# Value products as paired plain fp32, a second gate weight buffer, and compressed scores with both key parts in one product

## The chip, the cores and the metric

The kernel is one program on one core of one Trainium2 chip. Its engines are TensorE (PE in the profile, with its weight loads as PEld), VectorE (DVE), ScalarE (ACT), GpSimd (POOL) and the queue of SyncE (SP), which issues the DMAs. Each has its own list of instructions, worked off in order, and they meet at semaphores. The metric is the time of one launch on the device, in microseconds (us), from the median of several runs.

## The reference, cut to what matters

One decoder layer over 512 tokens of width 1024, all in fp32. Attention has 16 heads of 64 dims: eight block-sparse ones (MoBA; at this length every token sees its own and the earlier block, so they are causal attention) and eight NSA heads in two groups. An NSA head adds three branches: over 31 compressed blocks (`cmp`), over selected blocks (`slc`) and over a window (`win`), each with a gate of its own.

```python
h = rms_norm(x, attn_norm)
(mq, mk, mv, nsq, kc, vc, ksl, vsl, kwn, vwn, ngate, mgate) = split(h @ w_in)
y_a = softmax(q k^T * SCALE + bias) @ v                      # 8 MoBA heads
p_cmp = masked_softmax_safe(q kc^T * SCALE + bias)           # 31 compressed keys
o = gates[0] * (p_cmp @ vc) + gates[1] * o_slc + gates[2] * o_win   # 8 NSA heads
g_a, g_b = split(sigmoid(mgate))                             # 2 x 1024 columns
x = x + (g_a * (y_a @ w_br_moba) + g_b * (y_b @ w_br_nsa)) @ w_o
x = x + (gelu(conv_a) * conv_b) @ w_down                     # conv of rms_norm(x) @ w_up
x = x + sigmoid(x @ w_ple_gate) * (p @ w_ple)
```

## The kernel before, in words

**Arithmetic.** Most products are made of fp32r operands. Each fp32 operand is split into a high part (a copy rounded to fp32r) and a low part (the rest), and `three` (lines 1514 to 1518) issues high x high, high x low and low x high into one PSUM bank: three TensorE instructions for a product. Weights are split as they come in: the high part on ScalarE or VectorE, the low part on VectorE and GpSimd. Transposes and a few small products use plain fp32 operands (`L1604` for the hidden layer of the compression, `L1615` for its output, `L1701` for the warm-up). A plain fp32 product that is no transpose is one instruction in the program and two MATMUL records in the trace.

**Stages.** A prologue normalises and transposes x, projects the first head groups and compresses keys and values. Then comes attention, a loop over 100 steps (`STEPS`). After it the branch matrices, `w_o`, the FFN and the last gate follow as one stream of weight chunks.

**Attention.** Heads go in eight pairs `n` (0 to 3 MoBA, 4 to 7 NSA), two heads `e` in each. A unit `u` is one head and one branch: four steps, one for each block `i` of 128 queries, against 128*(i+1) keys. A MoBA pair has 2 units (8 steps), an NSA pair 4 units and one `cmp` step for both heads (17 steps). A step's chain: `scores` (PE) fills a bank, `bias` (DVE, L1301) adds the bias and takes the row minimum, `exp` (ACT, L900), `invert` (DVE, L1318), `scale` (POOL, L711 or L714); three steps later `turn_probs` (PE, L1667) transposes the probabilities, `pt_high` (ACT, L925, `cmp`: L922) copies them out of PSUM as the high part, `pt_low` (DVE, L1336, `cmp`: L1332) makes the low part. Two steps after the unit's last transposes, `values` (PE) multiplies: 4 key blocks x `three`, over 512, 384, 256 and 128 query columns. All products of a pair add up in bank 6, heads on different partitions: the stationary operand is always 128 wide, 64 columns of values and 64 of zeros, so that one head's product adds zeros to the other's half.

The values themselves are split by `v_high` (ACT, L866 for MoBA, four times L872 for an NSA pair) and `v_low` (POOL, L688, or four times L693).

**Compressed scores.** For each of 4 query blocks and 2 heads, `scores` makes two products of 32 columns, with the high keys `KCh` and the low keys `KCl` (L1641, L1642): 16 instructions per `cmp` step.

**Work between.** TensorE fills the steps with the projections of the next pairs (`PROJ`) and with 14 of the 16 blocks of the merge gates (`GATE`, L1516 to L1518 on bank 7; in pairs 6 and 7 a gate is 24 matmuls spread over four steps, then two steps without gate work follow). There is one gate weight buffer, `Gh`/`Gl`. At the step after gate `j` ends, ScalarE empties bank 7 (`take_gate`, L932) and then writes `Gh` for gate `j+1` (L1013), and VectorE (L1200) and GpSimd (L679) each make half of `Gl`. Gate `j+1` waits for that.

**Order.** Nothing is scheduled by a planner: the tables `PROJ`, `SPLIT`, `VALUES`, `GUESS`, `ROOT`, `TILE`, `TURN`, `GATE`, keyed by step, say at which step each engine does what beside the softmax chain.

## Time and profile before

| | |
|---|---|
| median of 3 runs | 921.58 us |
| lowest, highest | 920.68, 921.92 us |
| the profiled execution | 921.52 us |
| its span, first to last instruction | 919.7 us |
| TensorE clock granted, mean | 0.996 |
| attention loop | about 88 to 394 us of the span |
| TensorE busy in it | 286.9 of 306 us |

The profiled execution is as long as the median (0.06 us less), and 1.8 us of it lie outside the span. Rows of the trace give the start and length of instructions. A matmul's length includes its latency, and the next one starts before it ends: what a matmul costs in a dense stream is the distance from its start to the next start.

### The profile page before, as it was taken

How to read it: one execution, taken by the hardware profiler on the slowest of the kernel's cores; microseconds unless marked ns; L12 is line 12 of the kernel's file. 1: busy time of each engine (PE TensorE's matmuls, PEld its weight loads, DVE VectorE, ACT ScalarE, POOL GpSimd, SP SyncE). 2: the span in 40 equal slices, each digit the busy share in tenths (PEclk: the TensorE clock that was granted, in tenths of full speed). 3: DMA queues.
4: the chain of work that ended last, by engine and by line, in shares of the span. 5: the costliest groups of instructions: out<-in, count | busy, mean ns of one | idle time of the engine just before them, and what ended most of it. 6: DMA issues, size and time to landing. Idle time of an engine off the chain costs nothing.

```text
span 919.7 us, 13404 instructions
## 1 busy us (share of the span) xinstructions
PE 884.6 (96%) x4601; PEld 764.8 (83%) x4601; DVE 423.9 (46%) x961; ACT 411.8 (45%) x893; POOL 437.0 (48%) x557
## 2 busy tenths in 40 slices
PE   7999899999899799999999999999999999999998
PEld 7899699999798687877788888888888888888886
DVE  4545665767755654545413644444444440021124
ACT  5224555665646454634333544444444442231321
POOL 4740644664634342656462464444444445444450
PEclk9999999999999999999999999999999999999999
DMA  5845423333121223456532453333333333322213
GB/s 175 198 116 149 104 62 101 93 75 87 47 58 47 58 71 113 138 192 207 180 120 80 157 153 92 103 91 92 92 99 97 97 98 108 99 94 91 92 58 137
DMA packets 101366, 99.33 MB, mean 108 GB/s; under 512 B 15956, under 2 KB 76084, under 8 KB 101300
## 3 DMA queue, kind: packets, MB, share of 16 engines
q1 hardware_dynamic: 101247, 98.48, 36.5%
q8 instruction: 38, 0.62, 0.3%
q14 instruction: 28, 0.23, 0.1%
q10 hardware_dynamic: 53, 0.01, 0.0%
HBM read 87.58 MB, written 10.88 MB: 107 GB/s over the span
## 4 chain that ended last, share of the span: by engine, by line
PE 85%; DVE 5%; ACT 4%; issue 3%; POOL 2%; DMA 1%; SPq 0%; ACTq 0%; DVEq 0%; POOLq 0%
PE banks L1516 25%; PE banks L1517 25%; PE banks L1518 25%; PE banks L1667 2%; PE banks L1647 1%; PE banks L1646 1%; PE banks L1576 1%; PE banks L1604 1%; ACT split_arena L1013 1%; DMA plain_arena<-gates 1%; DMA plain_arena<-in_conv_w_dram 1%; ACT split_arena L889 1%; PE banks L1701 1%; DVE plain_arena L1301 1%; DVE split_arena L1200 1%
## 5 line engine op out<-in xcount | busy, mean ns | idle before, releaser
L1516 PE MATMUL banks<-split_arena 128*128 128x512 f32 (+4 forms) x1228 | 463.1, 377 | 12.8 <-DVE split_arena L1200 6.2
L1518 PE MATMUL banks<-split_arena 128*128 128x512 f32 (+4 forms) x1228 | 453.4, 369 | 0.0
L1517 PE MATMUL banks<-split_arena 128*128 128x512 f32 (+4 forms) x1228 | 453.3, 369 | 0.0
L699 POOL TENSOR_TENSOR split_arena<-plain_arena,split_arena 128x512 fp32r<-128x512 f32 x184 | 241.1, 1322 | 254.8 <-ACT split_arena L941 235.2
L1516 PEld LDWEIGHTS banks<-split_arena 128*128 128x128 f32 x1228 | 231.1, 188 | 50.9 <-DVE split_arena L1200 7.2
L1518 PEld LDWEIGHTS banks<-split_arena 128*128 128x128 f32 x1228 | 230.7, 188 | 35.4
L1517 PEld LDWEIGHTS banks<-split_arena 128*128 128x128 f32 x1228 | 231.3, 188 | 31.9
L941 ACT ACTIVATE split_arena<-plain_arena 128x512 fp32r<-128x512 f32 x184 | 113.0, 627 | 193.2 <-PE banks L1518 179.1
L1474 DVE SCALAR_TENSOR_TENSOR plain_arena<-banks,plain_arena 128x511 f32<-128x511 f32 x44 | 32.7, 743 | 133.2 <-ACT plain_arena L1053 133.2
L900 ACT ACTIVATE plain_arena<-plain_arena 128x128 f32<-128x128 f32 (+1 forms) x96 | 54.0, 562 | 52.7 <-DVE plain_arena L1301 52.4
L714 POOL TENSOR_SCALAR plain_arena<-plain_arena 128x128 f32<-128x128 f32 (+1 forms) x64 | 41.0, 641 | 74.4 <-DVE plain_arena L1318 74.4
L925 ACT ACTIVATE split_arena<-banks 128x128 fp32r<-128x128 f32 (+1 forms) x96 | 41.5, 433 | 66.7 <-PE banks L1667 57.9
L1301 DVE CUSTOM_DVE_ANT_0 plain_arena<-banks,plain_arena 128x128 f32<-128x128 f32 (+1 forms) x96 | 46.7, 486 | 47.0 <-PE banks L1647 46.8
L1336 DVE TENSOR_TENSOR split_arena<-banks,split_arena 128x128 fp32r<-128x128 f32 (+1 forms) x96 | 46.2, 482 | 15.1 <-ACT split_arena L925 14.0
L1667 PE MATMUL banks<-plain_arena 128*128 128x128 f32 x240 | 43.1, 278 | 2.4 <-DVE split_arena L1336 1.5
L1492 DVE TENSOR_TENSOR plain_arena<-banks,plain_arena 128x512 f32<-128x512 f32 x8 | 5.0, 683 | 86.5 <-PE banks L1518 86.5
L711 POOL TENSOR_SCALAR plain_arena<-plain_arena 128x128 f32<-128x128 f32 (+3 forms) x32 | 21.6, 674 | 46.2 <-DVE plain_arena L1318 45.7
L679 POOL TENSOR_TENSOR split_arena<-plain_arena,split_arena 128x512 fp32r<-128x512 f32 x16 | 26.6, 1665 | 35.3 <-DVE split_arena L1195 22.2
L675 POOL TENSOR_TENSOR split_arena<-plain_arena,split_arena 128x384 fp32r<-128x384 f32 (+1 forms) x28 | 31.3, 1122 | 19.6 <-ACT split_arena L841 10.1
L1053 ACT ACTIVATE plain_arena<-banks,plain_arena 128x512 f32<-128x512 f32 x44 | 30.6, 777 | 22.0 <-PE banks L1518 22.0
L1476 DVE SCALAR_TENSOR_TENSOR plain_arena<-banks,plain_arena 128x510 f32<-128x510 f32 x44 | 32.9, 749 | 1.5
L1667 PEld LDWEIGHTS banks<-plain_arena 128*128 128x128 f32 x240 | 28.8, 142 | 5.1 <-POOL plain_arena L714 3.1
(170 smaller groups left out, 821.7 us busy)
## 6 DMA issues: line engine op xcount, KB each, us to landing
plain_arena<-in_w_up_dram SPq DMA_DIRECT2D x88, 256.0 KB, 3.1
plain_arena<-in_w_down_dram SPq DMA_DIRECT2D x44, 256.0 KB, 2.6
plain_arena<-in_w_in_dram SPq DMA_DIRECT2D x18, 512.0 KB, 4.3
plain_arena<-in_w_in_dram SPq DMA_DIRECT2D x32, 192.0 KB, 4.2
plain_arena<-in_x_dram SPq DMA_DIRECT2D x8, 512.0 KB, 5.4
gates<-plain_arena SPq DMA_DIRECT2D x16, 256.0 KB, 2.0
plain_arena<-skew SPq DMA_DIRECT2D x16, 256.0 KB, 3.9
plain_arena<-gates SPq DMA_DIRECT2D x16, 256.0 KB, 4.2
```

Of the source, the lines that this page charges most:

```text
L699: pool.tensor_tensor(W2l[:, c % RING, :], raw2[:, c % RING, :], W2h[:, c % RING, :].bitcast(F32), ALU.subtract).then_inc(w2_lo, 1)
L714: pool.tensor_scalar(p_, p_, r, gsig[:, s["i"], h:h + 1], ALU.mult, ALU.mult).then_inc(scaled, 1)
L900: nc.scalar.activation(prob[:, t % 4, 0:nk], prob[:, t % 4, 0:nk], ACT.Exp, bias=mneg[:, t % 4:t % 4 + 1], scale=-1.0, accum_out=rsum[:, t ...
L925: nc.scalar.activation(PTh[:, s["u"] % 2, 0:i + 1, P * i:P * (i + 1)], PS[:, 4 + t % 2, 0:P * (i + 1)].rearrange("p (j q) -> p j q", j=i + ...
L941: nc.scalar.activation(W2h[:, c % RING, :], raw2[:, c % RING, :], ACT.Copy).then_inc(w2_hi, 1)
L1301: nc.vector.tensor_tensor_reduce(out=prob[:, t % 4, 0:nk], in0=PS[:, 2 + t % 2, 0:nk], in1=strip[:, n % 2, e, S - nk:S], scale=1.0, scalar ...
L1336: nc.vector.tensor_tensor(PTl[:, s["u"] % 2, 0:i + 1, P * i:P * (i + 1)], PS[:, 4 + t % 2, 0:P * (i + 1)].rearrange("p (j q) -> p j q", j= ...
L1476: nc.vector.scalar_tensor_tensor(out=dst[:, f % 2, 2:S], in0=PS[:, b, 0:S - 2], scalar=cst[:, CONVW + col:CONVW + 1 + col], in1=dst[:, f % ...
L1516: nc.tensor.matmul(o, ah, bh, start=first, stop=False)
L1517: nc.tensor.matmul(o, ah, bl, start=False, stop=False)
L1518: return nc.tensor.matmul(o, al, bh, start=False, stop=last)
L1667: ins = nc.tensor.transpose(PS[:, 4 + t % 2, P * j:P * (j + 1)], prob[:, t % 4, P * j:P * (j + 1)], ident)
```

## The change

The order of the steps changes: within a pair the branch is now the outer loop and the head the inner one, so both heads of a branch follow each other. A unit's values are no longer multiplied alone. `values` runs once for two units (`due`), on both heads. Its operands are plain fp32: `pt_low`, `v_high` and `v_low` are gone, ScalarE copies the probabilities as they are (`take_probs`, into four slots instead of two), and GpSimd copies the values once per pair (`take_values`). For each key block there are two matmuls of 64 output rows each, one head to partitions 0 to 63 and the other to partitions 64 to 127 of bank 6. The compressed values are one plain fp32 product instead of a `three`.

The gate weights get two buffers, taken in turn, and are split one gate earlier: at the end of gate `j` the weights of `j+2` are split, and one more split (gate 3) and one more load (gate 4) stand at steps 1 and 2. The compressed keys lie high and low side by side, so that one product of 64 columns gives both parts; VectorE adds them with one more instruction per `cmp` step.

```diff
-        for e in range(2):
-            for br in (["own"] if n < 4 else ["slc", "win"]):
+        for br in (["own"] if n < 4 else ["slc", "win"]):
+            for e in range(2):
...
-                if j > 0:
-                    dve.wait_ge(gate_filled, j)
-                nc.vector.tensor_copy(Gh, graw).then_inc(g_hi, 1)
+                if j > 1:
+                    dve.wait_ge(gate_filled, j - 1)
+                nc.vector.tensor_copy(Gh[j % 2], graw).then_inc(g_hi, 1)
...
                     if t == end + 1:
                         take_gate(j)
-                        if j + 1 < NGATE:
-                            act.wait_ge(graw_in, 16 * (j + 2))
-                            nc.scalar.activation(Gh, graw, ACT.Copy).then_inc(g_hi, 1)
+                        if j + 2 < NGATE:
+                            gate_high(j + 2)
+                if t == 1:
+                    gate_high(3)
...
+            def take_values(w):
                 n = w - 1
+                pool.wait_ge(qkv_done, 4 * w + 4)
+                if n >= 4:
+                    pool.wait_ge(pv_done, (n - 4) // 2 + 1)
+                pool.tensor_copy(V[:, vslot(n)], qkv[:, :, 256:384]).then_inc(v_done, 1)
...
-                            oq = o[:, P * q + 32 * e:P * q + 32 * e + 32]
-                            nc.tensor.matmul(oq, QQ[qslot(n)][:, e, P * q:P * (q + 1)], KCh[:, g, :], start=True, stop=False)
-                            ins = nc.tensor.matmul(oq, QQ[qslot(n)][:, e, P * q:P * (q + 1)], KCl[:, g, :], start=False, stop=True)
+                            oq = o[:, P * q + 64 * e:P * q + 64 * e + 64]
+                            ins = nc.tensor.matmul(oq, QQ[qslot(n)][:, e, P * q:P * (q + 1)], KC[:, g, :], start=True, stop=True)
...
-                    ins = three(PS[:, 6, :], VCh[:, g, :], VCl[:, g, :], PTh[:, u % 2, 0, :], PTl[:, u % 2, 0, :], False, closing)
+                    ins = nc.tensor.matmul(PS[:, 6, :], VC[:, (n - 4) // 2, :], PT[:, u % 4, 0, :], start=False, stop=closing)
                 else:
-                    vs = vslot(n, s["br"])
-
-                    for j in (reversed(range(NT)) if closing else range(NT)):
-                        q = slice(P * j, S)
-                        ins = three(PS[:, 6, q], Vh[:, vs, j, c0:c0 + P], Vl[:, vs, j, c0:c0 + P], PTh[:, u % 2, j, q], PTl[:, u % 2, j, q],
-                                    opening and j == 0, closing and j == 0)
+                    for j in range(NT):
+                        for h in range(2):
+                            c0 = DH * (h if n < 4 else s["br"] == "win")
+                            ins = nc.tensor.matmul(PS[DH * h:DH * (h + 1), 6, P * j:S], V[:, vslot(n), j, c0:c0 + DH], PT[:, (u - 1 + h) % 4, j, P * j:S],
+                                                   start=opening and j == 0, stop=closing and j == NT - 1)
                 ins.then_inc(pv_done, 1)
```

TensorE in an NSA pair, the value products. Before, this piece stands after each unit; it is one unit of one head, twelve matmuls on all 128 output rows.

```order
L1516 MATMUL banks<-split_arena 128x512
L1517 MATMUL banks<-split_arena 128x512
L1518 MATMUL banks<-split_arena 128x512
L1516 MATMUL banks<-split_arena 128x384
L1517 MATMUL banks<-split_arena 128x384
L1518 MATMUL banks<-split_arena 128x384
L1516 MATMUL banks<-split_arena 128x256
L1517 MATMUL banks<-split_arena 128x256
L1518 MATMUL banks<-split_arena 128x256
L1516 MATMUL banks<-split_arena 128x128
L1517 MATMUL banks<-split_arena 128x128
L1518 MATMUL banks<-split_arena 128x128
```

The same place in the changed kernel, with the scores (L1612, L1613) and the transposes (L1633) of the running step ahead of it.

```order
L1612 MATMUL banks<-attention_split 128x128
L1613 MATMUL banks<-attention_split 128x128
L1633 MATMUL banks<-plain_arena 128x128 x2
L1655 MATMUL banks<-attention_plain 64x512 x2
L1655 MATMUL banks<-attention_plain 64x384 x2
L1655 MATMUL banks<-attention_plain 64x256 x2
L1655 MATMUL banks<-attention_plain 64x128 x2
```

Twelve matmuls per unit, 24 for two heads, have become eight for both heads, each of 64 output rows, and they stand at every second place only.

GpSimd in steps 1 to 3 of attention, in the kernel before: the last of the root iterations (L724 to L730), scales (L711), low parts of the projection weights (L675) and of the values (L688).

```order
L728 TENSOR_SCALAR plain_arena<-plain_arena 128x8
L730 TENSOR_TENSOR plain_arena<-plain_arena 128x8
L711 TENSOR_SCALAR plain_arena<-plain_arena 128x256
L675 TENSOR_TENSOR split_arena<-plain_arena,split_arena 128x384
L688 TENSOR_TENSOR split_arena<-plain_arena,split_arena 128x4x2x64
L711 TENSOR_SCALAR plain_arena<-plain_arena 128x384
L675 TENSOR_TENSOR split_arena<-plain_arena,split_arena 128x384
```

The same in the changed kernel (L681 is the gate's low part, L704 the scale, L677 the projection weights, L688 the copy of the values).

```order
L721 TENSOR_SCALAR plain_arena<-plain_arena 128x8
L723 TENSOR_TENSOR plain_arena<-plain_arena 128x8
L681 TENSOR_TENSOR attention_split<-plain_arena,attention_split 128x512
L704 TENSOR_SCALAR plain_arena<-plain_arena 128x256
L677 TENSOR_TENSOR split_arena<-plain_arena,split_arena 128x384
L688 COPY attention_plain<-plain_arena 128x512
L704 TENSOR_SCALAR plain_arena<-plain_arena 128x384
L677 TENSOR_TENSOR split_arena<-plain_arena,split_arena 128x384
```

The gate's low part now stands ahead of the scale of step 1 and of the projection weights of step 2; the subtraction on the values has become a copy.

## Rows read from the trace of the kernel before

**Rows 1.** The page: busy time by engine (us, share of span, instructions).

```profile
PE 884.6 (96%) x4601; PEld 764.8 (83%) x4601; DVE 423.9 (46%) x961; ACT 411.8 (45%) x893; POOL 437.0 (48%) x557
```

**Rows 2.** Busy time by stretch: length, then each engine's busy us, PE clock, DMA share.

```profile
88.00:116.00 28.00, 23.55 (x134) 20.89 (x133) 17.71 (x47) 16.46 (x42) 16.45 (x36) 1.00 0.44 117
116.00:207.00 91.00, 90.55 (x550) 84.85 (x549) 61.14 (x170) 54.93 (x149) 50.00 (x109) 1.00 0.34 83
207.00:302.00 95.00, 87.92 (x553) 79.52 (x552) 60.03 (x198) 55.60 (x162) 45.19 (x97) 1.00 0.20 58
302.00:394.00 92.00, 84.91 (x489) 73.44 (x489) 51.98 (x178) 52.32 (x145) 38.33 (x49) 0.98 0.30 95
```

**Rows 3.** Waits of PE, 88 to 394 us: us in total, times, longest.

```profile
PE banks L1516 <- DVE split_arena L1200: 6.2, 5, 1.5
PE banks L1576 <- DVE plain_arena L1268: 5.2, 4, 2.8
PE banks L1516 <- DVE split_arena L1184: 3.1, 2, 1.7
```

**Rows 4.** Timeline of PE, one value unit (start, us, line, form, count).

```profile
151.51 0.48 PE L1516 MATMUL banks<-split_arena 128*128 128x512 f32 x1
151.83 0.39 PE L1517 MATMUL banks<-split_arena 128*128 128x512 f32 x1
152.06 0.40 PE L1518 MATMUL banks<-split_arena 128*128 128x512 f32 x1
152.30 0.33 PE L1516 MATMUL banks<-split_arena 128*128 128x384 f32 x1
...
153.45 0.39 PE L1516 MATMUL banks<-split_arena 128*128 128x384 f32 x1
```

**Rows 5.** Timeline of PE, plain fp32 products of the compression.

```profile
53.60 3.68 PE L1604 MATMUL banks<-plain_arena 128*128 128x62 f32 x32
...
74.38 0.34 PE L1518 MATMUL banks<-split_arena 128*128 128x384 f32 x1
74.65 0.63 PE L1615 MATMUL banks<-plain_arena 128*31 128x64 f32 x8
```

**Rows 6.** Timeline of PE, one step of compressed scores (first, last, next).

```profile
308.53 0.26 PE L1641 MATMUL banks<-split_arena 128*128 128x32 f32 x1
...
310.21 0.26 PE L1642 MATMUL banks<-split_arena 128*128 128x32 f32 x1
310.32 0.44 PE L1667 MATMUL banks<-plain_arena 128*128 128x128 f32 x2
```

**Rows 7.** Timeline of all engines at a gate that waits for its weights.

```profile
312.23 0.62 ACT L932 ACTIVATE plain_arena<-banks 128x512 f32<-128x512 f32 x1
...
312.71 1.08 ACT L1013 ACTIVATE split_arena<-plain_arena 128x1024 fp32r<-128x1024 f32 x1
...
314.57 0.50 PE L1516 MATMUL banks<-split_arena 128*128 128x512 f32 x1 [1.43 <-DVE split_arena L1200]
```

**Rows 8.** Timeline of POOL and PE at the longest wait.

```profile
294.55 2.83 POOL L693 TENSOR_TENSOR split_arena<-plain_arena,split_arena 128x256 fp32r<-128x256 f32 x4 [1.64 <-ACT split_arena L872]
297.35 0.67 POOL L714 TENSOR_SCALAR plain_arena<-plain_arena 128x384 f32<-128x384 f32 x1
...
302.16 1.09 PE L1576 MATMUL banks<-plain_arena 128*128 128x128 f32 x4 [2.84 <-DVE plain_arena L1268]
```

**Rows 9.** Groups by line: busy us, mean ns of one, idle before.

```profile
L1336 DVE TENSOR_TENSOR split_arena<-banks,split_arena 128x128 fp32r<-128x128 f32 (+1 forms) x96 | 46.2, 482 | 15.1 <-ACT split_arena L925 14.0
L900 ACT ACTIVATE plain_arena<-plain_arena 128x128 f32<-128x128 f32 (+1 forms) x96 | 54.0, 562 | 52.7 <-DVE plain_arena L1301 52.4
L925 ACT ACTIVATE split_arena<-banks 128x128 fp32r<-128x128 f32 (+1 forms) x96 | 41.5, 433 | 66.7 <-PE banks L1667 57.9
L679 POOL TENSOR_TENSOR split_arena<-plain_arena,split_arena 128x512 fp32r<-128x512 f32 x16 | 26.6, 1665 | 35.3 <-DVE split_arena L1195 22.2
L807 POOL COPY plain_arena<-plain_arena 128x512 f32<-128x512 f32 x1 | 0.6, 612 | 2.2 <-ACT plain_arena L1096 2.2
```

198 lines of the change are left out of this document (79 added, 119 removed).

## Prediction

> **What bounds the kernel now.** First the busy times of the page [rows 1]: TensorE is busy 884.6 of 919.7 us, no other engine over 48%. Busy time of a matmul includes latency, so this alone doesn't prove a bound. Next the attention loop by stretches [rows 2]: 286.9 of 306 us, with 0.45 us free between 116 and 207 us and some 4.5, 7 and 7 us in the other three. So TensorE sets the pace in attention, with about 19 us of holes. Then the waits of TensorE [rows 3]: 6.2 us of them are for the low part of gate weights (L1200), 5.2 us for the normalised queries and keys (L1268), 3.1 us for projection weights (L1184). What follows attention is the same stream of chunks in both kernels, and I give it no change: all terms lie in attention, and one that shortens TensorE's list there, or a wait of it, moves the end by as much, until a softmax chain comes last instead.
>
> **Value products, before.** One unit runs from 151.51 us to the next product at 153.45 us: 1.94 us for twelve matmuls [rows 4]. The 512-column ones follow each other at 0.235 us. There are 4 x 2 + 4 x 4 = 24 units: 46.6 us.
>
> **Value products, after.** Twelve calls (4 MoBA pairs, 2 for each of 4 NSA pairs), each 4 key blocks x 2 heads = 8 plain fp32 matmuls, which is 16 records, since a plain fp32 product leaves two. No row before shows a plain record of 512 columns. The bounds: the small product of the compression makes 8 records of 64 columns in 0.63 us [rows 5]. Less the last one's latency of about 0.22 that is 0.41 over 7 distances, 0.058 us for 64 columns, or 0.9 ns a column; fp32r takes 0.235 / 512 = 0.46 ns [rows 4]. One end is therefore the fp32r pace (0.235 us for 512 columns), the other twice that. The other rows of plain products don't decide it: 32 records of 62 columns take (3.68 - 0.27) / 31 = 0.11 us each [rows 5], as much as the 32-column fp32r records with their 128-wide weights [rows 6], so the weight load sets those. I take the slow end, 0.45, 0.34, 0.23 and 0.12 us for 512, 384, 256 and 128 columns, because L1615 is the only row in which the weights (31 wide) are too small to set the pace. A head's 8 records then take 2 x 1.14 = 2.28 us.
>
> The second unknown is whether the two heads' matmuls overlap, as they use different output rows of the array. Nothing before overlaps in that way. Fully overlapped, a call takes 2.28 us; if the records start in order, the second head begins one record late and a call takes 2.28 + 0.45 = 2.73 us; in series it takes 4.56 us. I take 2.5 us, and 0.2 us for two changes of the array's shape: from the last fp32r product to the first 31-wide one there are 0.27 us where 0.17 is the usual step [rows 5]. So 12 x 2.7 = 32.4 us, a gain of **14.2 us**. In series it would be 12 x 4.76 = 57.1 us, a loss of 10.5 us. Why the overlap rather than the series: weight loads of one product already run beside the streaming of another (PEld is busy 764.8 us beside PE's 884.6 [rows 1]), so the array isn't one unit that a single instruction holds; but that is thin, and the series stays a rival. The Trainium skill, TensorEngine Tiling (Array Packing), section Tiling Modes, says that a 128x64 shape makes two tiles that load and multiply in parallel, and that changing the shape drains the engine; no run here shows the former. By it a call would be near 2.28 us plus the drains.
>
> **Compressed scores.** 16 records in 310.32 - 308.53 = 1.79 us, 0.112 each whatever their columns [rows 6]. Eight remain: 4 x 8 x 0.112 = **3.6 us** gained. VectorE gets one more addition per `cmp` step, 4 of some 0.45 us in all the loop, beside other work. **Compressed values:** three fp32r matmuls of 512 (0.70 us) become two plain records (0.90 at the slow end, 0.47 at the fast): **0.8 us** lost over four steps.
>
> **Gate weights.** At a gate's end ScalarE empties bank 7 (0.62 us, from 312.23), writes the high part (1.08 us), VectorE the low one, and TensorE starts at 314.57 after 1.43 us idle [rows 7]. With two buffers the weights of the next gate are ready by then, and the same instructions work for the one after it. All 6.2 us [rows 3] go: what is late next is the scores' chain, 0.6 (bias) + 0.75 (exp) + 0.16 + 0.65 (scale) = some 2.3 us against three steps, and a gate's first part of 1.4 us now covers it. Gain **6.2 us**. ScalarE's and SyncE's waits keep their lead: the load for gate j+2 is issued as many steps ahead of its split as before.
>
> **Less beside TensorE.** VectorE loses 96 low parts of 0.482 us, 46.2 us [rows 9], 15% of its time in the loop; they stood between the transposes and the next but one. At 294.55 GpSimd spends 2.83 us on four low parts of values, after 1.64 us waiting for ScalarE's high parts, and then the scale at 297.35 and the root iterations, the result of which TensorE awaits until 302.16 (2.84 us idle) [rows 8]. One copy of 0.61 us [L807, rows 9] takes their place: over 2 us sooner for that chain. TensorE arrives sooner there too, so I count only about half of the 5.2 + 3.1 us of such waits: **3 us** gained (bounds 0 and 8).
>
> **What it adds.** Gate 3 is now split at step 1: 1.66 us on GpSimd [L679, rows 9], 1.06 on ScalarE, 0.7 on VectorE. Queued behind it on GpSimd are the scale of step 1, a projection weight's low part and the first values; TensorE waits for the scale in step 4 and for the weights in the projection from step 4 on. This is the stretch from 88 to 116 us, where TensorE is free 4.5 of 28 us already [rows 2], so it isn't hidden well: **1.5 us** lost (bounds 0 and 2.8). The copy of the values (0.61 instead of 1.3 us) pays part of it back. Load 4 at step 2 holds SyncE's queue until gate 3's low part is made, with the raw weights of later projections behind it; those have several steps of lead.
>
> **Steps that get too short.** ScalarE needs 0.562 + 0.19 + 0.433 = 1.2 us a step [L900, L925, rows 9] and 1.7 us at each gate's end; TensorE's steps without gate, projection or values hold some 0.7 us, with values they held 1.9 more. Between bursts that now come at every eighth step rather than every fourth, short steps stand in a row. From 302 us on, ScalarE is busy 52.3 of 92 us [rows 2], so there is no bound on the mean, but I take off **4 us** of the 24 us of gains (bounds 0 and 8).
>
> **Sum.** 14.2 + 3.6 - 0.8 + 6.2 + 3 - 1.5 - 4 = 20.7 us. The profiled execution took 921.5 us, the same as the median: 921.5 - 20.7 = 900.8, say **901 us**.
>
> **Rivals.**
> *In series.* The two heads' matmuls don't overlap, and the pairing does nothing: -10.5 + 3.6 - 0.8 + 6.2 + 3 - 1.5 and no loss to short steps: 0.0, 921.5 us. For it: no row shows an overlap. Against it: nothing but weight loads running beside products.
> *Slower.* In series, and the weight loads of a 64-wide tile aren't hidden either. Such a load is half of the 0.11 us of a 128-wide one [rows 6]: 16 x 0.055 x 12 = 10.6 us more, 932 us. It decides as soon as more than about 0.04 us of each record's load shows. Against it: before, a stream of 512-column products goes at 0.235 us with a load in each [rows 4], of which nothing shows. The Trainium skill, TensorE: Matmul & The Clock Gate, section Part 3: Packing small matmuls, says that loads overlap matmuls in flight only when their row group differs, and here both heads use all rows. Before, all products use all rows and their loads do overlap, so the trace disagrees with it for full-width tiles.
> *Faster.* A plain record streams at the fp32r pace and the heads overlap: a call is 1.14 + 0.23 + 0.2 = 1.6 us, 13 us less, 888 us. Against it: L1615 [rows 5].
> *The softmax chain takes over.* The pairing works but the short steps give back twice what I took off and the early split costs 2.8 us: 906 us. This is inside my forecast's own range, 895 to 909.
>
> **Chances.** Forecast with its range 0.68, in series 0.18, slower 0.08, faster 0.06. Within 0.2% is what a measurement of this kernel can tell from no change: 919.7 to 923.4 us. In series falls on either side of that: 0.06 faster, 0.08 within, 0.04 slower. So faster 0.80, same 0.08, slower 0.12. The range goes from 891 (part of the faster case) to 922 us (the series).
>
> **What would show it.** The trace after should have plain 64-row products with starts of the second head's record within 0.05 us of one of the first head's, and about 2.7 us from a call's first record to the product behind it; 4.6 us would mean the series. Waits of TensorE for the gate's low part should be gone. The `cmp` scores should take 0.9 us. DVE's busy time should fall by about 47 us. The wait at 302 us should shrink, and its dip of the clock with it. Wrong would be: a pace of the plain records other than 0.45 us for 512 columns, waits of the transposes (for the scale) of more than 8 us in sum, or a new hole of several us before 116 us.

## The result, and the profile after

The changed kernel took **914.6 us** (912.67 to 917.26, four runs) against 921.75 us for the kernel before beside it: ratio 0.993, 95% interval 0.9915 to 0.9946. The change gains 7.1 us, about a third of the 20.7 us of the sum. The profiled execution is the slowest of the four, 917.26 us with a span of 915.3 us, so its trace shows only 4.3 us of gain; the readings below are differences inside the two traces, held against that.

The page after, busy time by engine, answers to [rows 1]:

```profile
PE 878.3 (96%) x4469; PEld 735.4 (80%) x4469; DVE 378.0 (41%) x864; ACT 406.7 (44%) x880; POOL 426.9 (47%) x547
```

VectorE lost 45.9 us, TensorE 6.3 us. The stretches of attention, answering to [rows 2] (length, busy us of PE, PEld, DVE, ACT and POOL, PE clock, DMA share, GB/s):

```profile
88.00:116.00 28.00, 22.50 (x118) 19.97 (x117) 15.63 (x41) 15.12 (x37) 17.43 (x37) 0.94 0.48 127
116.00:207.00 91.00, 90.57 (x550) 80.83 (x548) 50.40 (x154) 55.59 (x152) 48.01 (x112) 1.00 0.37 91
207.00:295.00 88.00, 82.88 (x504) 68.80 (x503) 45.30 (x161) 53.01 (x154) 40.74 (x89) 0.98 0.20 57
295.00:385.00 90.00, 78.49 (x422) 60.70 (x423) 37.64 (x146) 53.78 (x149) 39.25 (x49) 0.95 0.31 98
```

Two things are new: in the last 90 us TensorE is free for 11.5 us (7.1 of 92 before), and its granted clock is below 1.00 in three of four stretches. Together the clock column stands for 28 x 0.06 + 88 x 0.02 + 90 x 0.05 = 7.9 us of lost pace, against 92 x 0.02 = 1.8 us before. The window ends at 385 us and misses most of the last stretch at the lower clock, 383.7 to 387.1 us. With it there are five such stretches of 3.4 us in attention, 17.1 us in all, of which half is lost: 8.5 us, against one stretch and 1.7 us before. The waits of TensorE from 88 to 385 us, answering to [rows 3] (us in total, times, longest):

```profile
PE banks L1483 <- ACT plain_arena L911: 5.7, 3, 2.1
PE banks L1543 <- DVE plain_arena L1248: 4.8, 4, 2.0
PE banks L1483 <- POOL split_arena L790: 4.6, 1, 4.6
PE banks L1483 <- DVE split_arena L1164: 2.8, 2, 2.2
```

The gate's low part (L1200 before) is gone from the list. In its place stand L911, ScalarE emptying the gate's bank 7, with 5.7 us, and L790, GpSimd's first low part of y, with one wait of 4.6 us at the end of attention. L1248 and L1164 are the lines that were L1268 and L1184.

A call of the paired value products in the timeline of TensorE (start, us, form, count), answering to [rows 4]:

```profile
136.41 0.40 PE L1633 MATMUL banks<-plain_arena 128*128 128x128 f32 x2
136.74 2.38 PE L1655 MATMUL banks<-attention_plain 128*64 128x512 f32 x16
139.05 0.44 PE L1483 MATMUL banks<-split_arena 128*128 128x384 f32 x1
```

From 136.74 to 139.05 us are 2.31 us for both heads; all twelve calls take 2.30 or 2.31. A plain fp32 product leaves two records, here called its first and second pass. Inside a call the records start in pairs, 7 ns apart: the first pass of both heads, then the second pass of both. A pass of 512 columns takes 0.43 us to the next start. And the compressed scores, answering to [rows 6]:

```profile
300.64 1.06 PE L1608 MATMUL banks<-attention_split 128*128 128x64 f32 x8
301.53 0.33 PE L1633 MATMUL banks<-plain_arena 128*128 128x128 f32 x1
```

0.89 us, as forecast. So both mechanisms of the change work as described; what became of their gain is the question of the experiments.

Why TensorE waits for L911, in the timeline of all engines after (in brackets: idle before, and what ended it):

```profile
301.53 0.77 PE L1633 MATMUL banks<-plain_arena 128*128 128x128 f32 x5
301.74 0.42 DVE L1289 TENSOR_TENSOR plain_arena<-banks,plain_arena 128x256 f32<-128x256 f32 x1 [0.94 <-PE banks L1608]
...
303.11 0.42 DVE L1292 TENSOR_TENSOR plain_arena<-plain_arena 128x256 f32<-128x256 f32 x1
...
303.57 0.42 ACT L876 ACTIVATE plain_arena<-plain_arena 128x256 f32<-128x256 f32 x1 [0.29 <-DVE plain_arena L1292]
...
303.89 0.58 ACT L911 ACTIVATE plain_arena<-banks 128x512 f32<-128x512 f32 x1
...
304.61 0.47 PE L1483 MATMUL banks<-split_arena 128*128 128x512 f32 x1 [2.14 <-ACT plain_arena L911]
```

The bank has been full since about 299.5 us. ScalarE empties it only behind the exponential L876 of the compressed step, which waits for VectorE's four-operation bias chain (L1289 to L1292, one addition longer than before), which waits for the scores. Before the change the same order held, but the low part of the next weights came later still, and hid it.

Behind attention the kernels were to be equal. They aren't. The groups of matmuls in the dn stage, before (748 to 870 us) and after (740 to 865 us), columns as in [rows 9]:

```profile
L1516 PE MATMUL banks<-split_arena 128*128 128x512 f32 x177 | 69.0, 390 | 0.0
```

```profile
L1483 PE MATMUL banks<-late_arena,split_arena 128*128 128x512 f32 x176 | 69.6, 396 | 0.0
```

A matmul is 6 ns longer on average; from start to start it is 233.5 ns instead of 226.7, and the stage takes 123.3 us instead of 119.8. In the up stage, with the same shape, both kernels go at 226.7 ns (239.5 us). From the first transpose of x to the up stage it is 81.5 instead of 80.3 us. So 4.7 us go behind attention.

### The profile page after: what moved, and what is told of

It reads as the page before. It is cut to its first block, busy times and chain, and to the rows that moved or that the text cites. A ratio compares the mean times of both kernels' runs of the same rounds, so it can differ in the third digit from the quotient of the medians.

```text
span 915.3 us, 13019 instructions
## 1 busy us (share of the span) xinstructions
PE 878.3 (96%) x4469; PEld 735.4 (80%) x4469; DVE 378.0 (41%) x864; ACT 406.7 (44%) x880; POOL 426.9 (47%) x547
## 4 chain that ended last, share of the span: by engine, by line
PE 86%; DVE 4%; ACT 3%; issue 3%; POOL 2%; DMA 1%; SPq 1%; ACTq 0%; DVEq 0%; POOLq 0%
PE banks L1483 25%; PE banks L1485 25%; PE banks L1484 25%; PE banks L1655 3%; PE banks L1633 2%; PE banks L1613 1%; PE banks L1612 1%; PE banks L1543 1%; PE banks L1571 1%; PE banks L1663 1%; DMA plain_arena<-in_conv_w_dram 1%; ACT attention_split L868 1%; DVE plain_arena L1281 0%; ACT plain_arena L879 0%; POOL split_arena L677 0%
## 5 line engine op out<-in xcount | busy, mean ns | idle before, releaser
L692 POOL TENSOR_TENSOR split_arena<-plain_arena,split_arena 128x512 fp32r<-128x512 f32 x184 | 240.9, 1321 | 263.3 <-ACT split_arena L925 243.7
L1483 PE MATMUL banks<-split_arena 128*128 128x512 f32 (+3 forms) x808 | 305.6, 378 | 12.4 <-POOL split_arena L790 4.6
L1485 PE MATMUL banks<-split_arena 128*128 128x512 f32 (+3 forms) x808 | 297.7, 368 | 0.0
L1484 PE MATMUL banks<-split_arena 128*128 128x512 f32 (+3 forms) x808 | 297.3, 368 | 0.0
L1483 PEld LDWEIGHTS banks<-split_arena 128*128 128x128 f32 x808 | 152.8, 189 | 38.2 <-POOL split_arena L790 4.8
L1485 PEld LDWEIGHTS banks<-split_arena 128*128 128x128 f32 x808 | 152.7, 189 | 21.5
L1484 PEld LDWEIGHTS banks<-split_arena 128*128 128x128 f32 x808 | 153.1, 189 | 20.3 <-issue 0.5
L1483 PE MATMUL banks<-late_arena,split_arena 128*128 128x512 f32 x240 | 95.2, 397 | 0.0
L1485 PE MATMUL banks<-late_arena,split_arena 128*128 128x512 f32 x240 | 94.8, 395 | 0.0
L1484 PE MATMUL banks<-late_arena,split_arena 128*128 128x512 f32 x240 | 94.8, 395 | 0.0
L707 POOL TENSOR_SCALAR plain_arena<-plain_arena 128x128 f32<-128x128 f32 (+1 forms) x64 | 40.8, 639 | 72.3 <-DVE plain_arena L1299 72.3
L904 ACT ACTIVATE attention_plain<-banks 128x128 f32<-128x128 f32 (+1 forms) x96 | 41.6, 433 | 69.6 <-PE banks L1633 69.4
L1485 PEld LDWEIGHTS banks<-late_arena,split_arena 128*128 128x128 f32 x240 | 45.0, 187 | 11.1
L1484 PEld LDWEIGHTS banks<-late_arena,split_arena 128*128 128x128 f32 x240 | 45.0, 187 | 10.8
L1483 PEld LDWEIGHTS banks<-late_arena,split_arena 128*128 128x128 f32 x240 | 45.0, 188 | 10.8
L1633 PE MATMUL banks<-plain_arena 128*128 128x128 f32 x240 | 43.2, 281 | 1.2 <-POOL plain_arena L707 1.2
L677 POOL TENSOR_TENSOR split_arena<-plain_arena,split_arena 128x384 fp32r<-128x384 f32 (+1 forms) x28 | 32.7, 1173 | 22.5 <-ACT split_arena L836 12.9
```

The lines of the kernel that those rows point to most:

```text
L677: pool.tensor_tensor(Wl[:, kt, 0:c], raw[:, kt, 0:c], Wh[:, kt, 0:c].bitcast(F32), ALU.subtract).then_inc(w_lo[1], 1)
L692: pool.tensor_tensor(W2l[:, c % RING, :], raw2[:, c % RING, :], W2h[:, c % RING, :].bitcast(F32), ALU.subtract).then_inc(w2_lo, 1)
L707: pool.tensor_scalar(p_, p_, r, gsig[:, s["i"], h:h + 1], ALU.mult, ALU.mult).then_inc(scaled, 1)
L904: nc.scalar.activation(PT[:, u % 4, 0:i + 1, P * i:P * (i + 1)], PS[:, 4 + t % 2, 0:P * (i + 1)].rearrange("p (j q) -> p j q", j=i + 1), A ...
L1483: nc.tensor.matmul(o, ah, bh, start=first, stop=False)
L1484: nc.tensor.matmul(o, ah, bl, start=False, stop=False)
```

## The experiments

Each comparison of times is with the kernel before on the same chip; the kernel after is 914.6 us throughout. For each run the trace also gives, from the first scores to the first transpose of x, the sum of TensorE's gaps of 0.35 us or more and the time at the lower clock (1.2 GHz, seen in pieces of 3.4 us; a piece that begins within 0.3 us of that transpose is counted). Half of such a piece is lost where TensorE works through it, and less where it waits anyway. Both columns come from one execution each:

| kernel | us | ratio to before, 95% | gaps | us at 1.2 GHz |
|---|---|---|---|---|
| before | 921.8 | | 21.4 | 3.4 |
| after | 914.6 | 0.9915 to 0.9946 | 22.8 | 17.1 |
| a_serial | 931.6 | 1.0094 to 1.0131 | 21.0 | 13.7 |
| a_onegate | 921.9 | 0.9992 to 1.0027 | 26.5 | 30.7 |
| a_gate3late | 915.3 | 0.9917 to 0.9947 | 22.4 | 23.9 |
| a_takefirst | 909.7 | 0.9862 to 0.9903 | 20.7 | 13.7 |
| b_takefirst | 922.1 | 0.9999 to 1.0018 | 20.7 | 13.7 |
| a_invfirst | 914.9 | 0.9917 to 0.9944 | 21.2 | 23.9 |
| a_ylow | 915.2 | 0.9905 to 0.9942 | 21.8 | 20.5 |
| a_endgap | 912.6 | 0.9881 to 0.9921 | 20.1 | 17.1 |
| a_align | 912.5 | 0.989 to 0.994 | 22.1 | 13.7 |
| b_shift | 921.9 | 0.9995 to 1.0026 | 20.4 | 10.2 |
| a_rel14272 | 910.7 | 0.9861 to 0.9912 | 23.4 | 17.1 |
| a_best | 904.9 | 0.9793 to 0.9835 | 18.8 | 10.2 |
| a_best2 | 902.9 | 0.9781 to 0.9825 | 19.0 | 13.7 |
| a_best3 | 900.6 | 0.9754 to 0.9784 | 16.2 | 10.2 |

The last column changes between executions of the same instructions. b_shift only places the data elsewhere and has two pieces that the trace of before lacks; a_ylow differs from the kernel after only at the end of attention, and yet has a piece at 98 us that the kernel after lacks. One or two pieces (1.7 or 3.4 us of time) between two rows are therefore not shown to come from the edit. That the change as such lowers the clock is better founded: its four runs have a mean granted clock of 0.988 to 0.991, and 47 runs of the kernel before have 0.992 to 0.998.

### Is it the pairing? a_serial

```diff
-                    for j in range(NT):
-                        for h in range(2):
+                    for h in range(2):
+                        for j in range(NT):
```

> The kernel after, with the value products of a call in the order of the heads: all four key blocks of the first head (output rows 0 to 63), then all four of the second (rows 64 to 127), instead of the two heads in turn. The same 8 products and 16 records a call. Theory E (two products run side by side only when they stand next to each other and differ in their 64 columns of the array): a call takes twice as long, 4.4 us or a little more instead of 2.3 us, TensorE's stream grows by 12 x 2.1 = 25 us, and the time is 20 to 27 us above the kernel after (935 to 941 us), which is the prediction's rival in series with its 4.6 us a call. Rival F (plain products into 64 rows are cheap in themselves, side by side or not): a call stays at 2.3 to 2.7 us and the time at 914 to 918 us.

931.55 us, 16.9 us above the kernel after. The call:

```profile
136.66 3.93 PE L1655 MATMUL banks<-attention_plain 128*64 128x512 f32 x16
140.52 0.44 PE L1483 MATMUL banks<-split_arena 128*128 128x384 f32 x1
```

3.86 us instead of 2.31. Theory E holds in kind: the same records take 1.55 us less when the two heads stand next to each other, 12 x 1.55 = 18.6 us in all. In size it missed: the call isn't twice as long, because at the one seam a rest of the overlap is there: the second head's two 512-column passes start beside the first head's last 256-column and 128-column ones. The second head's eight records alone take 2.30 us, as long as the whole paired call. Without the pairing the change would have cost 10 us.

### Is it the gates split one gate earlier? a_onegate

```diff
-                    if t == end + 1 and j + 2 < NGATE:
-                        split_gate(j + 2)
-                if t == 1:
-                    split_gate(3)
+                    if t == end + 1 and j + 1 < NGATE:
+                        split_gate(j + 1)
```

(and the same on SyncE, ScalarE and VectorE; both weight buffers stay)

> The kernel after, with the gate weights loaded and split one gate ahead, as in the kernel before, instead of two (no split of gate 3 at step 1), into the same two alternating buffers. By the prediction, two gates ahead is worth 6.2 us of waits less 1.5 us for the early split: this kernel would be 4.7 us slower than the kernel after (919 us). By the traces since, where the waits for the low part have given way to waits for the emptying of bank 7 and for the scale chain: within 1.5 us of the kernel after. If the early split does more harm than the second buffer good, it is faster than the kernel after, and the two gaps of TensorE from 98 to 108 us are smaller.

921.86 us: 7.3 us slower than after, and the same as before. From the first scores to the first transpose of x it is 3.1 us shorter than the kernel before (335.7 for 338.8 us), where the kernel after is 9.2 us shorter; the slower pace behind attention, below, takes the 3.1 us and more. TensorE's list in attention, counted from start to start without gaps and without what the lower clock adds, falls from 315.0 to 295.6 us there, about as in the kernel after (296.7 us). But its gaps of any length are 5.5 us longer than before and the lower clock costs 10.8 us more, so 3 of 19 us are left. The waits of TensorE in that kernel:

```profile
PE banks L1475 <- DVE attention_split L1174: 8.8, 4, 3.7
PE banks L1475 <- POOL split_arena L786: 4.6, 1, 4.6
PE banks L1475 <- DVE split_arena L1174: 4.5, 2, 3.7
```

The low part of the gate weights (L1174 here) now costs 13.3 us where it cost 6.2 [rows 3], and four of the gaps have 6.8 us at the lower clock behind them. The work on ScalarE and VectorE ahead of a gate is the same, but TensorE arrives sooner, since its list is shorter. My 1.5 us "by the traces since" was wrong, since I had compared with before's 6.2 us; the prediction's 4.7 us were nearer, and also too small. No run has the two gate buffers without the rest of the change, so what they would gain alone on the kernel before is not shown.

### The early split: a_gate3late

```diff
-                if t == 1:
-                    split_gate(3)
+                if t in (4, 8):
+                    split_gate(3 if t == 4 else 4)
```

(and the same on the other engines; from step 10 on as in the kernel after)

> The kernel after, with the weights of gates 3 and 4 split at steps 4 and 8 instead of 1 and 4; from step 10 on two gates ahead as in the kernel after. Theory I (the early split of gate 3 is what opens the 2.0 and 2.25 us gaps at 98 and 106 us, by keeping GpSimd from the roots of the normalisation): the gaps of TensorE from 95 to 110 us fall from 5.5 us to the 3.8 us of the kernel before or less, and the time falls by 1 to 3 us against the kernel after (912 to 913.5 us). Rival J (the work only moves, to a gap behind step 8): the same sum of gaps up to 130 us and the same time within 1 us.

915.32 us, no change. Theory I was right on the place: the gaps from 95 to 110 us are 0.72, 1.75 and 0.66, sum 3.1 us instead of 5.5. A new one of 1.15 us appears at 125 us, behind step 8, as in rival J. And behind the same two gaps of 2.1 and 4.6 us at the end there are now 6.8 us at the lower clock each, not 3.4, which in this execution takes the rest back. Alone the edit shows no gain.

### What took the gate's place: a_takefirst and b_takefirst

```diff
             for t in range(T + LAG):
+                for j, end in gate_end.items():
+                    if t == end + 1:
+                        take_gate(j)
                 for done in proj_end(t):
...
                     if t == end + 1:
-                        take_gate(j)
```

> The kernel after, with ScalarE emptying the gate's bank at the start of the step behind the gate's end, ahead of that step's copies of probabilities and its exponential, instead of behind them. Theory C (the emptying of bank 7 is what is late where the low part of the weights had been): TensorE's 5.7 us of waits for L911 go to under 1 us, at least two of the five dips of the clock in attention go with them (each costs some 1.7 us), and the time falls by 3 to 6 us against the kernel after. Rival D (the wait only covers another: the scores' chain, behind which ScalarE stood, is late as well): the waits turn up at the transposes or score banks, the sum of the gaps of TensorE from 15 to 400 us stays at 22 to 25 us, and the time changes by less than 1.5 us either way.

909.65 us, 5.0 us under the kernel after: theory C. The waits for the emptying are gone, and at the place quoted above TensorE now goes on after 0.40 us:

```profile
301.76 0.66 PE L1635 MATMUL banks<-plain_arena 128*128 128x128 f32 x4 [0.40 <-POOL plain_arena L707]
302.17 0.47 PE L1485 MATMUL banks<-split_arena 128*128 128x512 f32 x1
```

The lower clock behind the gaps near 237, 305 and 343 us is gone in this execution, though 3.4 us more stand at the end of attention and 3.4 us near 411 us. Part of rival D holds too: the waits for L1250 (the normalised vectors) rise from 4.8 to 6.4 us.

> The kernel before, with ScalarE emptying the gate's bank at the start of the step, ahead of its other work (the edit of a_takefirst, on the kernel without the change). If that edit is worth as much there, 5 us (916 us), the gain of a_takefirst has nothing to do with the change. By the traces: in the kernel before TensorE waited at the gates for the low part of the weights, 6.2 us, which is made behind the high part that stands behind the emptying; taking it first moves the high part little, so the gain should be 0 to 2 us (919 to 922 us).

922.07 us, 0.9999 to 1.0018 of before: the edit is worth nothing there. So the emptying of the bank became late only through the change.

### The gap at the end of attention: a_invfirst, a_ylow, a_endgap

Instructions of three engines stand in front of the first product behind attention. These runs moved them one after the other: VectorE's reciprocals ahead of the bias in compressed steps; then GpSimd's first low part of y ahead of the last scale and of a fill; then VectorE's low part of y behind the last bias.

```diff
+                early = 1 <= t < T and STEPS[t]["br"] == "cmp"
+                if early:
+                    invert(t - 1)
                 if t < T:
                     bias(t)
-                if 1 <= t <= T:
+                if 1 <= t <= T and not early:
                     invert(t - 1)
```

> The kernel after, with VectorE taking the reciprocals of the step before ahead of the bias chain in the five-operation steps of the compressed branch (4 steps), instead of behind it. Theory G (the 4.58 us gap of TensorE at the end of attention is that reciprocal: GpSimd's scale waits for it, and the last low parts of y stand behind the scale on GpSimd): that gap falls by 1.5 to 2 us, to 2.5 to 3 us, and the time by 1 to 3 us against the kernel after (912 to 913.5 us). Rival H (the gap is ScalarE's high parts or GpSimd's own work, 4 x 0.6 us and more): the gap stays over 4 us and the time within 1 us of the kernel after.

914.86 us; the gap falls from 4.58 to 3.82 us, half of what theory G wanted, and it is still GpSimd that ends it. No gain.

```diff
+                if t == T - 1:
+                    pool.wait_ge(gate_filled, NGATE)
+                    pool.wait_ge(yt_hi, 1)
+                    pool.tensor_tensor(yTl[:, 0, :], ytmp[:, 0, :], yTh[:, 0, :].bitcast(F32), ALU.subtract).then_inc(yt_lo[0], 1)
                 if t >= 1:
                     scale(t - 1)
```

> The kernel after, with GpSimd writing the first low part of y (needed by the first product behind attention) ahead of the scale of the last but one step, instead of behind that scale and behind a fill that waits for the bias of the last step. Theory K (the 4.6 us gap at the end of attention is the queue in front of that one instruction: reciprocal, scale, bias of the compressed step, fill): the gap falls from 4.6 to under 2 us, the time by 2.5 to 5 us against the kernel after (910 to 912 us), the half-speed stretch of the clock behind it with it. Rival L (the next thing, ScalarE's high part of y or the scores' chain of the last steps, is nearly as late): the gap stays over 3 us, the time within 1.5 us of the kernel after.

915.2 us; rival L. The gap is 3.96 us and has another last waiter, the emptying of the last gate's bank, again behind the exponential of the compressed step:

```profile
381.10 0.47 PE L1486 MATMUL banks<-split_arena 128*128 128x512 f32 x1 [3.96 <-ACT plain_arena L914]
```

With that emptied first (a_best2, below), the gap is still 4.03 us, and the timeline shows the next in line:

```profile
368.60 1.27 POOL L767 TENSOR_TENSOR split_arena<-plain_arena,split_arena 128x512 fp32r<-128x512 f32 x1 [0.73 <-ACT split_arena L1012]
369.01 1.41 DVE L1375 TENSOR_TENSOR split_arena<-plain_arena,split_arena 128x512 fp32r<-128x512 f32 x1 [1.90 <-ACT split_arena L1012]
370.35 0.15 DVE L1304 RECIPROCAL plain_arena<-plain_arena 128x1 f32<-128x1 f32 x1
370.42 0.40 DVE L1294 TENSOR_TENSOR plain_arena<-banks,plain_arena 128x256 f32<-128x256 f32 x1
...
371.77 1.12 DVE L1297 TENSOR_TENSOR plain_arena<-plain_arena 128x256 f32<-128x256 f32 x1
...
373.23 0.76 PE L1491 MATMUL banks<-split_arena 128*128 128x512 f32 x1 [4.03 <-DVE plain_arena L1297]
```

The last bias chain (L1294 to L1297) had its scores at 368.6 us, and stood behind VectorE's own low part of y, which takes 1.41 us beside GpSimd's and 0.69 alone.

```diff
-                if T - 2 <= t < T + 1:
-                    m = 2 * (t - T + 2) + 1
+                for m in {T - 1: (1, 3), T: (5,)}.get(t, ()):
```

> The kernel after with the edits of a_invfirst and a_ylow and one more: VectorE writes its low part of y (1.4 us there, since GpSimd works beside it) behind the last bias chain instead of ahead of it. Theory M (the gap at the end of attention is the bias chain of the last step, which stood in VectorE's queue behind the low part of y; with 4.6, 3.8 and 4.0 us in turn three queues were equally late): the gap falls from 4.0 to about 2.5 us or less, with one stretch of half clock behind it less, and the time by 2 to 5 us against the kernel after (910 to 912.5 us). Rival N (the emptying of the gate's bank on ScalarE, or the product's own operands, are as late again): the gap stays over 3.5 us and the time at 914 to 916 us.

912.62 us with all three moves: the gap is 2.73 us, and the lower clock behind it is gone (another piece stands at 99 us instead, so their sum is that of the kernel after). Theory M, at the low end of its gain: 2.0 us, and the intervals of the two kernels still overlap. ScalarE's emptying of the bank ends this gap, and in a_best3, where that is first, 1.96 us are left:

```profile
372.07 0.47 PE L1490 MATMUL banks<-split_arena 128*128 128x512 f32 x1 [1.96 <-DVE plain_arena L1297]
```

So the 4.6 us had four causes, each hidden behind the one in front: GpSimd's queue, the reciprocals, the emptying of the bank and VectorE's low part of y. The first two, each removed alone, brought no time.

### The pace behind attention: a_align, b_shift, a_rel14272

```diff
-        F = ctx.enter_context(nc.sbuf_tensor("plain_arena", [P, 14280], F32))
+        F = ctx.enter_context(nc.sbuf_tensor("plain_arena", [P, 14288], F32))
```

> The kernel after, with plain_arena 8 columns (32 bytes a partition) longer, so that attention_plain, attention_split and late_arena begin at a multiple of 64 bytes instead of 32 bytes past one. Nothing else changes. Theory A (start of the moving operand): in the dn stage, whose moving operand gT stands in late_arena, the three matmuls of a product follow each other at 234 ns in the kernel after and at 227 ns in the kernel before, 1/32 of 213 ns apart, as if a 512-column operand that begins 32 bytes off took one 64-byte piece more. By it this kernel's dn stage takes 119.8 us instead of 123.3 us, the wo stage about 1 us less, and the whole is 4 to 6 us under the kernel after (about 909 to 911 us). Rival B (the operand's place in another arena, far up in memory, or the drained state after attention, costs the 7 ns): dn stays at 234 ns and 123.3 us, and the time stays at 914 to 917 us.

912.5 us. The dn stage takes 121.0 us: its three matmuls follow each other at 232, 226 and 229 ns. In part what theory A wanted.

The kernel before with plain_arena ahead of split_arena:

```diff
-        R = ctx.enter_context(nc.sbuf_tensor("split_arena", [P, 38912], F32R))
         F = ctx.enter_context(nc.sbuf_tensor("plain_arena", [P, 14280], F32))
+        R = ctx.enter_context(nc.sbuf_tensor("split_arena", [P, 38912], F32R))
```

> The kernel before, with plain_arena laid out ahead of split_arena, so that split_arena, which holds nearly all moving operands of TensorE, begins 32 bytes past a multiple of 64. Nothing else changes. Theory A (start of the moving operand): every fp32r product of 512 columns takes some 6.7 ns more, dn goes from 119.8 to about 123.3 us and up from 239.5 to about 246.5 us, the whole is 15 to 24 us slower than before (937 to 946 us). Rival B (it is another property of the new arenas): no stage changes, within 1 us of 921.6 us.

921.91 us, dn 119.8, up 239.5 us: no stage moved, although every moving operand in split_arena now begins 32 bytes past a multiple of 64. Theory A is wrong: the start alone doesn't matter.

```diff
-        F = ctx.enter_context(nc.sbuf_tensor("plain_arena", [P, 14280], F32))
+        F = ctx.enter_context(nc.sbuf_tensor("plain_arena", [P, 14272], F32))
```

> The kernel after, with plain_arena 8 columns shorter (14272, its last columns are unused), so that late_arena begins 122,624 bytes behind split_arena: a multiple of 256 bytes. In the kernel after that distance is 122,656 (96 modulo 128), in the run with aligned arenas 122,688 (64 modulo 128). In the kernel before gT and the ring of weights stood in one arena, 32,768 bytes apart, with or without the shift of the whole arena. Theory A2 (what counts is the distance in memory between the moving operand gT and the weights read beside it, modulo 128 bytes or more, not either's own start): the dn stage returns to 226 or 227 ns a matmul and 119.8 us, the whole is 3 to 5 us under the kernel after (910 to 912 us). Rival B (late_arena as such costs something): dn stays at 121 to 123.3 us.

910.67 us (two runs, 908.75 and 912.6), 3.9 us under the kernel after; the stages show it more surely than the times. The same group as above:

```profile
L1483 PE MATMUL banks<-late_arena,split_arena 128*128 128x512 f32 x176 | 68.6, 389 | 0.0
```

dn takes 119.8 us, and the stretch ahead of the up stage 80.2 us, both as before. Three distances between gT and the ring of its weights are thus measured: 32 modulo 128 bytes (233.5 ns a matmul; 122,656 is 32 modulo 128, and the 96 in the expectation is a slip), 64 (229), 0 (226.7). In the kernel before and in b_shift the distance is 0 modulo 128 too, at 226.7 ns. In these five placements the pace goes with the distance, and no start of the moving operand alone explains it. That it is the weight reads beside the stream that collide is my reading, which no run shows.

### All of it: a_best, a_best2, a_best3

a_best has four edits: plain_arena at 14272 columns, the gate's bank first, the reciprocals first, the later splits of gates 3 and 4. a_best2 adds the move on GpSimd, a_best3 the one on VectorE.

> The kernel after, with four things at once: plain_arena 8 columns shorter (as in a_rel14272), ScalarE emptying the gate's bank first (as in a_takefirst), the reciprocals ahead of the compressed branch's bias (as in a_invfirst), and the weights of gates 3 and 4 split at steps 4 and 8 instead of 1 and 4, from step 10 on two gates ahead as in the kernel after. If the separate gains add up: 5 us for the bank, 3 us for dn, 1.5 us for the last gap, 1 to 2 us for the hole near 100 us: 903 to 906 us. If the gaps only move, as they did between the gate's waits, and the dips of the clock stay: 907 to 910 us.

> The kernel of a_best with the first low part of y ahead of the scale, as in a_ylow. In a_best the gap at the end of attention was still 3.8 us, with a stretch of 6.8 us at half clock behind it. By theory K both shrink: 899 to 902 us. By rival L: 903 to 905 us, as a_best.

> The kernel of a_best2 with VectorE's low part of y behind the last bias chain. Here the gate's bank is emptied first already, and the last bias was what TensorE waited for (4.0 us, with 6.8 us of half clock behind it). By theory M: the gap 2.5 us or less, 899 to 901.5 us. By rival N: 902 to 904 us.

904.86, 902.86 and 900.57 us. Made together, the edits give more than alone: the four of a_best gave 5.0 and 3.9 us and nothing in single runs, and 9.7 us here. a_best3 is 14.0 us under the kernel after and 2.3% under before (0.9754 to 0.9784), the best of all kernels here. Its last two stretches of attention:

```profile
207.00:295.00 88.00, 82.90 (x504) 68.64 (x502) 45.90 (x160) 53.17 (x154) 40.40 (x88) 0.98 0.18 53
295.00:372.00 77.00, 71.99 (x405) 54.46 (x403) 34.98 (x135) 49.08 (x139) 36.52 (x45) 1.00 0.34 108
```

5.0 us are free in the last stretch instead of 11.5, at the full clock. a_best2 missed theory K (its gap stayed at 4.0 us, as told above); a_best3 hit theory M.

## Why the prediction failed, by its own steps

What bounds the kernel was read rightly, and so was the direction; 914.6 us lies inside the range and outside the forecast's own 895 to 909.

**Value products.** -14.2 us forecast. A call takes 2.305 us and its first record starts 0.20 us behind the last transpose, where a 128-wide product starts 0.03 us behind one, so the shape change costs 0.17 us: 12 x 2.48 = 29.7 us for 46.6, **-16.9 us**. The pace of 0.43 us for 512 columns is near the slow end I took (0.45), and the overlap is complete, where I had taken 2.5 us, between overlapped (2.28) and one record late (2.73). The Trainium skill, TensorEngine Tiling (Array Packing), section Tiling Modes, which the prediction weighed, says that different tiles load and multiply in parallel and that a change of the mode drains the engine; the records 7 ns apart and the 0.17 us agree with both.

**Compressed scores** -3.6 us, as measured. **Compressed values**: 0.46 us a step instead of the 0.90 taken, about -1 us instead of +0.8.

**Gate weights, -6.2 us: the step that failed first.** "What is late next is the scores' chain ... and a gate's first part of 1.4 us now covers it" left out an instruction that the prediction itself had named a few sentences earlier, ScalarE emptying bank 7. It stood in ScalarE's queue behind that very chain, so it inherits the chain's lateness in full. L1200's 6.2 us went and L911's 5.7 us came: **-0.5 us** at this point. But the term's meaning was also wrong: a_onegate shows the earlier split, which the second buffer allows, to be worth 7.3 us in the changed kernel, not against the waits of before but against those that the shorter stream would have made. The terms for pairing and gates were added as if independent, and they aren't: without the earlier split the pairing leaves 3.1 us in attention. That most of what the split gains is the pairing's is argued from this; the split without the pairing was not run.

**Less beside TensorE, -3 us.** The waits for normalised vectors outside the first hole fell from 5.2 to 2.8 us: **-2.4 us**. The chain at 295 us came sooner, as read from [rows 8].

**Early split, +1.5 us**: the gaps from 95 to 110 us grew from 3.8 to 5.5 us, **+1.7**, and moving the split alone gained nothing.

**Steps too short, +4 us: mis-sized.** The gap at the end of attention grew from 1.3 to 4.6 us, +3.3, and the lower clock costs 8.5 instead of 1.7 us, +6.8: **+10.1 us**. I had written that the dip of the clock would shrink with the wait near 302 us. That wait did shrink, to 1.2 us at 295 us, and its dip went. But there is now a dip behind each of five other gaps of 1.4 to 4.6 us, at 111, 237, 305, 343 and 384 us. A gap doesn't always bring one: none follows the gap of 2.0 us at 101 us, nor any of seven gaps of 1.3 to 1.7 us in the trace of before. What decides it is not shown. The granted clock (last but two of the columns) behind two of the gaps:

```profile
305.00:309.00 4.00, 4.00 (x15) 3.42 (x14) 2.63 (x10) 1.98 (x6) 2.22 (x2) 0.57 0.29 83
343.00:346.50 3.50, 3.50 (x13) 2.92 (x13) 2.47 (x8) 1.56 (x4) 1.78 (x1) 0.55 0.23 82
```

**Behind attention, 0: wrong by 4.7 us.** "What follows attention ... I give it no change" took the same instructions for the same time. The change had moved gT and mT to another arena; a_rel14272 gives 3.9 us back by moving it 32 bytes. Why the distance counts stays open.

The sum of what was found is -16.9 - 3.6 - 1.0 - 0.5 - 2.4 + 1.7 + 10.1 + 4.7 = -7.9 us, against -7.1 measured by the medians and -4.3 between the two profiled executions, from which these terms are read. So 3.6 us are not placed. Most of them lie in TensorE's list in attention, which got 18.3 us shorter (315.0 to 296.7 us) and not 16.9 + 3.6 + 1.0 = 21.5. That the sum comes near the medians is luck: the profiled execution of the kernel after is the slowest of its four.

**The rivals.** In series was wrong (2.3 us a call, not 4.6), though its result, 921.5 us, is what a_onegate took, for another reason. "The softmax chain takes over" at 906 us was the right kind, and too small. What would show it: VectorE's 46 us, the compressed scores and the lost waits for the low part came as said. The sum of the waits for the scale rose only from 0.8 to 1.2 us (L714, then L707), so this warning sign didn't come: it wasn't the scale that was late, but an unrelated instruction queued behind the chain.

## What to carry to other kernels

When TensorE's list gets shorter between two of its waits, those waits can grow by as much, up to the next engine's chain (here from 6.2 to 13.3 us in a_onegate): price a shorter list and a removed wait together, and ask for each wait that goes what stands right behind it in each queue, first of all the instructions that empty a bank and have nothing to do with the chain ahead of them. Such instructions belong at the head of a step's queue; moving this one was worth 5 us after the change and nothing before it. And when a change lays out the memory anew, compare the start-to-start pace of one untouched stage before adding up the terms.

## What the runs showed of the hardware

- Plain fp32 products into output rows 0 to 63 and 64 to 127, issued in turn, run fully side by side: 16 records in 2.31 us, as long as one head's 8 records alone (2.30 us in a_serial), against 3.86 us when one head's follow the other's.
- The pace of a 512-column fp32r product went with the distance between the moving operand and the weights that are loaded beside it: 226.7 ns at 0, 229 at 64 and 233.5 at 32 modulo 128 bytes. A shift of both together changes nothing. The Trainium skill, TensorE: Matmul & The Clock Gate, section Part 2: What happens when you issue a matmul, says that loading the next weights takes no read bandwidth from the running product. The 6.8 ns a matmul that come and go with the distance speak against it, if the collision is the one I read into them.
- Two subtractions of 512 columns, one on VectorE and one on GpSimd: VectorE's took 1.41 us in a_best2, where GpSimd's ended at 369.87 us and VectorE's 0.55 us later, as if it had stood still until then. In the kernel after, with GpSimd idle, it took 0.69 us:

```profile
379.01 0.69 DVE L1367 TENSOR_TENSOR split_arena<-plain_arena,split_arena 128x512 fp32r<-128x512 f32 x1 [1.91 <-ACT split_arena L1007]
```

- The same gap of 4.6 us at the end of attention was followed by 3.4 us at 1.2 GHz in the kernel after and by 6.8 us in a_gate3late and a_takefirst. Gains of 1 to 2 us can't be told from this; the 5.0 us of a_takefirst and the kernels with several edits can.
